# First attention in residue-class order with four key blocks a head, first scores among the transposes, and two more buffers for the late modulation units

## The chip, the cores and the metric

The kernel runs on one core of a Trainium2 chip. The metric is the device time of one execution in microseconds (us), the median of several runs.

## What is computed

One launch computes a whole layer of 256 tokens by 1024 channels, and then a second layer (a mixer, a memory cross-attention and a mixture of experts). The change touches only the middle of the first layer. What matters of its reference:

```python
DIL_GROUPS = ((128, 1), (512, 4), (2048, 16))      # (window, dilation); 4 heads of 64 channels in each group
...
def dilated_window_attention(q, k, v, window, dilation):
    """Each query i attends to keys i + dilation*m, |m| <= window/(2*dilation)."""
...
    mod = jax.nn.silu(c) @ w_ada + b_ada            # six rows of 1024, used to shift, scale and gate
    h = rms_norm(x, norm1_g) * (1 + sc1) + sh1
    proj = h @ w_in
    qa, ka, va, qb, kb, vb, gl = jnp.split(proj, IN_SPLITS, axis=-1)
    ...
    for gi, (win, dil) in enumerate(DIL_GROUPS):    # first attention: 12 heads
        o, l = dilated_window_attention(qa[:, :, sl], ka[:, :, sl], va[:, :, sl], win, dil)
    ...
    oa = softmax over the three groups' lse, times their outputs, summed
    branch_a = oa.reshape(b, s, DIL_OUT) @ w_proj_a
    ob = differential_attention(q1, q2, k1, k2, vb, lam)   # second attention: 8 heads
```

With 256 tokens, the group of dilation 4 reaches every key of the query's class modulo 4, and the group of dilation 16 every key of its class modulo 16. Only the group of dilation 1 has a band (64 tokens to either side). The three groups' softmax and the mixing by their denominators come to one softmax over the concatenated scores of one head of each group.

## The kernel before, in words

Weights come as units of 128 x 2048 numbers (1 MB) from one stream in memory. SP issues the loads. For a weight in TensorE's split precision, ACT makes a rounded copy (`hi`, L721), DVE the rest (`lo`, L1278), and TensorE (PE) multiplies three times (`mm3`, L2389 to L2391). Every engine runs an order that is written out by hand, with semaphores between them.

The stage around the change is this. The projection ends with unit U_PA - 1. Then PE transposes the queries and keys of both attentions (L2580), four blocks of 128 x 128 to a PSUM bank, 14 groups `g`; ACT copies the even groups to `qkT` (L871), DVE the odd ones (L1586). The last wait before the first scores is for all 14 copies.

The first attention has 8 steps `i` (4 slots, 2 halves of 128 queries; one step takes one head of each of the three groups). Of a step:
- `a_scores(i)` (PE, L2598): three products of 128 queries by 256 keys, 768 score columns in two PSUM banks
- `a_mask(i)` (DVE, L1594, L1597, L1599): scale and add the mask, take the maximum, negate it
- `a_exp(i)` (ACT, L877): the exponential in place, with the sum
- `a_transposes(i)` (PE, L2609): six 128 x 128 transposes to banks 4 and 5, which are free only when the step before has been copied
- the copy of these (ACT, L885), 768 columns, `a_pT`
- `a_values(i)` (PE, L2619): six products with the values, accumulated in bank 6
- `a_inverse(i)` (L1607) and `a_rows(i)` (L1613) on DVE: one over the sum, and the output rows

PE's order in step `i` is transposes(i), scores(i + 2), values(i - 1), `ada_half(1, i + 1)`. DVE's is inverse(i), `ada_sum(8 + i)`, mask(i + 2), rows(i - 1). In the last two steps the second attention's scores (L2631) and maxima (L1619, L1623) stand in for scores and mask. Before step 0, PE does scores(0), scores(1) and `ada_half(1, 0)`.

`ada_half` (L2496) and `ada_sum` (L1358, and L1360 for the first of eight) work off the late modulation units: 16 units `k` = 0 to 15 of the matrix `w_ada`, one in each step of the first attention and one in each of the 8 heads of the second (`ada_half(2, h)`, `ada_sum(16 + h)`). PE takes some columns of a unit, DVE the rest. These units lie in the two buffers `raw[:, 0 or 1, :]`; SP issues the load of unit `k` (L571) when both engines are done with `k - 2`. Behind unit 15 come U_PA and U_PB, the weights of the next products, into `spare` (L574), and further units into `raw` (L580). U_PA needs `hi`, `lo`, and then the transposed first attention (`T_OA`: ACT L768, DVE L1295) before PE goes on.

The second attention's heads begin on DVE with `b_weights` (L1647 to L1653). Its PE work is scores (L2631), transposes (L2662), values (L2674) and `ada_half`.

The masks are built by DVE between the projection's `lo` operations (L1446 to L1455). POOL only issues a few DMAs here. `H` (128 x 2 x 1024) is free from the first transposes of the projection until `b_rows` of the second attention writes it.

## Time and profile before

| | |
|---|---|
| median of 3 runs | 1825.12 us (1824.62 to 1835.89) |
| the profiled execution | 1830.13 us, of which the span is 1828.3 us |
| PE, DVE, ACT, POOL busy | 98%, 74%, 52%, 11% of the span |
| mean granted TensorE clock | 0.996 of full speed |
| PE transposes of queries and keys begin | 199.0 us after the span's start |
| step 0 of the first attention begins on PE | 211.0 us |
| the second attention's `b_weights(0)` begins on DVE | 249.8 us |
| PE's first product with U_PA | 289.2 us |

Times in the text are us from the start of the span. Busy shares are averages over the whole program; the rows further down are of the 90 us that the change touches.

### The profile page before, as it was taken

To read this page: it belongs to the slowest core of one execution; us is meant where nothing else is said; L and a number is where in the kernel's file an instruction comes from. 1 tells how busy PE (TensorE), PEld (TensorE's weight loads), DVE (VectorE), ACT (ScalarE), POOL (GpSimd) and SP (SyncE) were. 2 spreads that over 40 slices of the span, in tenths; PEclk is the share of its full clock that TensorE was granted. 3 is DMA by queue.
4 is the path that set the end of the run, shared out by engine and by line. 5 is a ranking of instruction groups with operands and counts; after the bars stand their busy time and mean duration, and the time that the engine had idled before them with its cause. 6 is when DMAs were issued, how large, how long until landed. Compare 5 with 4: busy or idle time off the path is not lost.

```text
span 1828.3 us, 25528 instructions
## 1 busy us (share of the span) xinstructions
PE 1791.1 (98%) x10036; PEld 1530.1 (84%) x10036; DVE 1355.7 (74%) x1887; ACT 952.2 (52%) x1035; POOL 197.5 (11%) x165
## 2 busy tenths in 40 slices
PE   8999999999999999999999999999999999999998
PEld 3788766899999988888888888898979888888886
DVE  5679687679589966666666666667874788888897
ACT  2543564454444444444444444456644567667665
POOL 0000000187700014441000000000000000000000
PEclk9999999999999999999999999999999999999999
DMA  8655365564445468886555555555343688898894
GB/s 316 253 184 185 132 224 188 199 234 174 185 157 205 188 235 276 289 293 225 185 195 193 184 186 195 193 189 182 134 151 145 237 329 344 332 353 330 324 354 171
DMA packets 65296, 413.55 MB, mean 226 GB/s; under 512 B 8641, under 2 KB 8929, under 8 KB 18865
## 3 DMA queue, kind: packets, MB, share of 16 engines
q1 hardware_dynamic: 51904, 371.22, 55.0%
q0 software_dynamic: 7248, 25.01, 4.0%
q10 hardware_dynamic: 6050, 16.02, 2.2%
q8 instruction: 64, 1.05, 0.2%
q14 instruction: 30, 0.25, 0.0%
HBM read 395.45 MB, written 16.78 MB: 225 GB/s over the span
## 4 chain that ended last, share of the span: by engine, by line
PE 88%; DVE 6%; DMA 3%; ACT 2%; issue 1%; SPq 0%; DVEq 0%; ACTq 0%
PE ps L2389 23%; PE ps L2391 22%; PE ps L2390 22%; PE ps L2766 6%; PE ps L2795 3%; PE ps L2768 3%; DVE wlo L1278 2%; DMA BIG<-in_stream_dram 1%; ACT whi L721 1%; PE ps L2978 1%; DMA raw<-in_stream_dram 1%; PE ps L2496 1%; PE ps L2619 1%; PE ps L2598 1%; PE ps L2856 1%
## 5 line engine op out<-in xcount | busy, mean ns | idle before, releaser
L1278 DVE TENSOR_TENSOR wlo<-raw,whi 128x2048 fp32r<-128x2048 f32 x181 | 414.7, 2291 | 208.4 <-ACT whi L721 208.2
L721 ACT ACTIVATE whi<-raw 128x2048 fp32r<-128x2048 f32 x181 | 346.8, 1916 | 368.3 <-PE ps L2391 241.7
L2389 PE MATMUL ps<-whi,phi 128*128 128x512 f32 x608 | 238.1, 392 | 2.3 <-DVE plo L1874 2.3
L2391 PE MATMUL ps<-whi,plo 128*128 128x512 f32 x608 | 237.2, 390 | 0.0
L2390 PE MATMUL ps<-wlo,phi 128*128 128x512 f32 x608 | 237.1, 390 | 0.0
L2389 PE MATMUL ps<-whi,tboth 128*128 128x512 f32 (+1 forms) x576 | 227.3, 395 | 6.9 <-DVE wlo L1278 4.0
L2389 PE MATMUL ps<-tboth,whi 128*128 128x256 f32 x768 | 221.6, 289 | 2.9 <-DVE tboth L1295 2.8
L2391 PE MATMUL ps<-whi,tboth 128*128 128x512 f32 (+1 forms) x576 | 223.9, 389 | 0.0
L2390 PE MATMUL ps<-wlo,tboth 128*128 128x512 f32 (+1 forms) x576 | 223.6, 388 | 0.0
L2391 PE MATMUL ps<-tboth,wlo 128*128 128x256 f32 x768 | 217.7, 283 | 0.0
L2390 PE MATMUL ps<-tboth,whi 128*128 128x256 f32 x768 | 217.7, 283 | 0.0
L2766 PE MATMUL ps<-tboth,whi 128*128 128x512 f32 x480 | 169.4, 398 | 0.0
L2389 PEld LDWEIGHTS ps<-tboth,whi 128*128 128x128 f32 x768 | 147.4, 192 | 4.2 <-issue 4.2
L2390 PEld LDWEIGHTS ps<-tboth,whi 128*128 128x128 f32 x768 | 147.5, 192 | 0.0
L2391 PEld LDWEIGHTS ps<-tboth,wlo 128*128 128x128 f32 x768 | 147.3, 192 | 0.0
L2389 PEld LDWEIGHTS ps<-whi,tboth 128*128 128x128 f32 x576 | 108.7, 189 | 32.8 <-DVE wlo L1278 5.2
L2389 PEld LDWEIGHTS ps<-whi,phi 128*128 128x128 f32 x608 | 114.2, 188 | 26.0 <-issue 3.7
L2391 PEld LDWEIGHTS ps<-whi,plo 128*128 128x128 f32 x608 | 114.2, 188 | 24.0
L2390 PEld LDWEIGHTS ps<-wlo,phi 128*128 128x128 f32 x608 | 114.3, 188 | 23.8
L2391 PEld LDWEIGHTS ps<-whi,tboth 128*128 128x128 f32 x576 | 108.6, 188 | 22.3
L2390 PEld LDWEIGHTS ps<-wlo,tboth 128*128 128x128 f32 x576 | 108.8, 189 | 21.6 <-issue 0.5
L2768 PE MATMUL ps<-tboth,wlo 128*128 128x256 f32 x420 | 118.1, 281 | 0.0
(435 smaller groups left out, 3313.3 us busy)
## 6 DMA issues: line engine op xcount, KB each, us to landing
raw<-in_stream_dram SPq DMA_DIRECT2D x249, 1024.0 KB, 4.8
BIG<-in_stream_dram SPq DMA_DIRECT2D x90, 1024.0 KB, 6.5
BIG<-g_spill POOLq DMA_DIRECT2D x64, 128.0 KB, 4.6
s_spill<-MOD ACTq DMA_DIRECT2D x28, 256.0 KB, 2.1
H<-in_stream_dram SPq DMA_DIRECT2D x6, 1024.0 KB, 4.9
BIG<-in_stream_dram SPq DMA_DIRECT2D x2, 2048.0 KB, 16.5
g_spill<-H ACTq DMA_DIRECT2D x4, 1024.0 KB, 5.4
g_spill<-MOD ACTq DMA_DIRECT2D x4, 1024.0 KB, 5.3
```

The source lines that it names most:

```text
L721: nc.scalar.activation(hi_of(u), raw_of(u), ACT.Copy).then_inc(unit_hi, 1)
L1278: nc.vector.tensor_tensor(wlo[:, u % 2, :], raw_of(u), whi[:, u % 2, :].bitcast(f32), ALU.subtract).then_inc(unit_split, 1)
L2389: nc.tensor.matmul(out, ahi, bhi, start=start, stop=False)
L2390: nc.tensor.matmul(out, ahi, blo, start=False, stop=False)
L2391: return nc.tensor.matmul(out, alo, bhi, start=False, stop=stop)
L2496: last = nc.tensor.matmul(ps[:, (7, 6)[g - 1] + m, :], silu_wide[:, c, :], raw[:, at % 2, m * 512:(m + 1) * 512], start=c == 0, stop=c == ...
L2598: last = nc.tensor.matmul(sc[:, k * S:(k + 1) * S], qkT[part, hd // 2, t * P:(t + 1) * P], qkT[part, 6 + hd // 2, :], start=True, stop=True)
L2619: last = nc.tensor.matmul(ps[:, 6, 0:HD], a_pT[b][:, k * P:(k + 1) * P], proj[:, k % 2, V0 + hd * HD:V0 + (hd + 1) * HD], start=k == 0, st ...
L2766: last = nc.tensor.matmul(out, whi[:, s, cols], both, start=c == 0, stop=c == DC - 1)
L2768: nc.tensor.matmul(out[:, 0:S], wlo[:, s, cols], thi[:, c, :], start=False, stop=False)
L2795: last = nc.tensor.matmul(out[:, q * N_KEYS:(q + 1) * N_KEYS], one_a[k][:, q, :], one_b[k][:, q, :], start=True, stop=True)
L2856: last = nc.tensor.matmul(ps[:, 4 + 2 * (l % 2) + t, h * P:(h + 1) * P], ks[:, h, kt * P:(kt + 1) * P], qs[:, h, qt * P:(qt + 1) * P], sta ...
```

## The change: what it does

1. **Class order.** Tokens are reordered by residue modulo 4, as the columns of `qkT` of the first attention: position (r, a) holds token 4a + r. The 128 queries of half `t` are then the classes 2t and 2t + 1. The groups of dilation 4 and 16 need only the 128 keys of the same half; the band group still takes all 256. A step has 512 score columns in one PSUM bank instead of 768 in two, four transposes instead of six, four products with the values instead of six. The transposes alternate between banks 4 and 5.
2. **Reordering costs.** The copies of the first six groups (blocks of the first attention's queries and keys) and the two operations of `T_OA` are strided (every fourth element). The values are moved into the new row order by eight DMAs on POOL, each 32 partitions by 768 numbers, from `proj` to `H`; they wait for the projection's block 12, and PE's first `a_values` waits for them (`v_moved`). The masks are built in the new order, with two small operations more and four operations of half the width.
3. **The sign.** The scores are negated with the masks, so that DVE's reduction is a minimum and is the bias itself; the operation on L1599 falls away, and `a_exp` has scale -1.
4. **The order before step 0.** After 8 of the 14 transpose groups PE waits for the copies of the first six and does scores(0) and scores(1); then the other six groups. DVE does mask(0) ahead of its copies 9, 11, 13; ACT does exp(0) behind its copy 8, ahead of copies 10 and 12.
5. **Buffers.** The late units 2, 3, 6, 7, 10 and 11 go to `late_units`, which lies over `whi` (free between the last unit of the projection and U_PA). Units 2 and 3 are issued when the projection's last units are used; units 4 to 13 when unit `k - 4` is used; units 14 and 15 when `k - 2` is used, as before.
6. **Semaphores.** `b_gate` and the late part of `b_ada` share one; DVE's block 7 waits for both.

The diff, cut to its core:

```diff
+CLASSES = A_DIL[1]
+QKT_FIRST, QKT_ALL = 8, QK_W // P // 4 * TT
...
+        with nc.sbuf_tensor("late_units", [P, 2, UW], f32) as late_tensor:
+            late_units = late_tensor
         whi = sb("whi", [P, 2, UW], f32r)
...
+        v_class = H[:, :, 0:A_W]
...
+        def by_class(cols):
+            return cols.rearrange("p c (a r) -> p c r a", r=CLASSES)
+        def qkT_rows(b4, t):
+            out, got = qkT[:, 4 * b4:4 * b4 + 4, :], ps[:, 4 + (TT * b4 + t) % 4, :].rearrange("p (b t) -> p b t", b=4)
+            if 4 * b4 >= 2 * A_W // P:
+                return out[:, :, t * P:(t + 1) * P], got
+            n = P // CLASSES
+            return out.rearrange("p b (r a) -> p b r a", r=CLASSES)[:, :, :, t * n:(t + 1) * n], by_class(got)
...
+        def late_of(at):
+            k = at - (U_PA - ADA_LATE)
+            return (late_units[:, at % 2, :] if k % 4 >= 2 and k < ADA_LATE - 2 else raw[:, at % 2, :])
...
             for u in range(late + 1, U_PA):
-                sp.wait_ge(unit_split, u - 1 - SPLIT_0)
-                if u - 2 >= late:
-                    sp.wait_ge(ada_used, u - 1 - late)
-                sp.dma_start(raw[:, u % 2, :], stream[u, :, :]).then_inc(raw_loaded[u % 2], 16)
+                k = u - late
+                if k >= 2:
+                    sp.wait_ge(raw_loaded[u % 2], landed(u - 2))
+                if k in (2, 3):
+                    sp.wait_ge(unit_used, U_PA - 4 + k - SPLIT_U + 1)
+                else:
+                    freed = u - 2 if k < 2 or k >= ADA_LATE - 2 else u - 4
+                    sp.wait_ge(unit_split, freed + 1 - SPLIT_0)
+                    if freed >= late:
+                        sp.wait_ge(ada_used, freed + 1 - late)
+                sp.dma_start(late_of(u), stream[u, :, :]).then_inc(raw_loaded[u % 2], 16)
...
+            pool.wait_ge(acc_free, 2 * ((V0 + A_W) // 512 + 1))
+            n = P // CLASSES
+            for r in range(CLASSES):
+                to, r2 = r // TT, r % TT * (P // 2)
+                for t in range(TT):
+                    pool.dma_start(v_class[r2 + t * n:r2 + (t + 1) * n, to, :], proj[r:P:CLASSES, t, V0:V0 + A_W]
+                                   ).then_inc(v_moved, 16)
...
+            for g in range(0, QKT_FIRST + 2, 2):
+                qkT_copy(g)
             a_exp(0)
+            for g in range(QKT_FIRST + 2, QKT_ALL, 2):
+                qkT_copy(g)
...
+                    if t == T_OA:
+                        nc.vector.tensor_tensor(by_class(tlo[:, chunks, tokens]), ps[:, tr_bank(t, k), :].rearrange(
+                            "p (c r a) -> p c r a", c=TT, r=CLASSES), by_class(thi[:, chunks, tokens].bitcast(f32)),
+                            ALU.subtract).then_inc(tr_lo, 1)
...
-                mark(nc.vector.scalar_tensor_tensor(a_s[b], sc, HD ** -0.5, masks[:, t * S:t * S + 768],
+                mark(nc.vector.scalar_tensor_tensor(a_s[b], ps[:, 2 * b, :], -(HD ** -0.5), masks[:, t * S:t * S + 512],
                                                     ALU.mult, ALU.add))
                 settle()
-                mark(nc.vector.tensor_reduce(a_max[:, b:b + 1], a_s[b], axis=AX.X, op=ALU.max))
-                settle()
-                nc.vector.tensor_scalar(a_nmax[:, b:b + 1], a_max[:, b:b + 1], -1.0, None,
-                                        ALU.mult).then_inc(a_masked, 1)
+                nc.vector.tensor_reduce(a_nmax[:, b:b + 1], a_s[b], axis=AX.X, op=ALU.min).then_inc(a_masked, 1)
...
+            for g in range(1, QKT_FIRST, 2):
+                qkT_copy(g)
             a_mask(0)
+            for g in range(QKT_FIRST + 1, QKT_ALL, 2):
+                qkT_copy(g)
             a_mask(1)
...
+                for g in a_groups(t):
+                    keys = rows if g else slice(0, S)
+                    n = keys.stop - keys.start
+                    last = nc.tensor.matmul(ps[:, 2 * b, at:at + n], qkT[part, hd // 2, rows],
+                                            qkT[part, 6 + hd // 2, keys], start=True, stop=True)
...
-                if i:
-                    pe.wait_ge(a_trT, i)
-                for k in range(6):
+                if i >= 2:
+                    pe.wait_ge(a_trT, i - 1)
+                for k in range(4):
...
+                else:
+                    pe.wait_ge(v_moved, 16 * CLASSES * TT)
                 pe.wait_ge(a_trT, i + 1)
...
+            for g in range(QKT_FIRST):
+                qkT_transposes(g)
+            pe.wait_ge(qkT_even, 2 * A_W // P // 4)
+            pe.wait_ge(qkT_odd, 2 * A_W // P // 4)
             a_scores(0)
             a_scores(1)
+            for g in range(QKT_FIRST, QKT_ALL):
+                qkT_transposes(g)
+            pe.wait_ge(qkT_even, QKT_ALL // 2)
+            pe.wait_ge(qkT_odd, QKT_ALL // 2)
             pe.wait_ge(silu_spread, 1)
             ada_half(1, 0)
```

## Rows read from the trace of the kernel before

**Rows 1.** Chain that ended last, from 199 us: start, duration, what, instructions.

```profile
199.15 6.13 PE ps L2580 x56
...
222.19 0.66 PE ps L2609 x6
222.85 1.49 PE ps L2598 x6
224.34 1.48 PE ps L2619 x12
225.82 0.91 PE ps L2496 x2
...
264.28 0.89 PE ps L2674 x8
...
271.23 4.85 DMA raw<-in_stream_dram
276.10 8.19 DMA spare<-in_stream_dram
...
288.55 0.61 DVE tboth L1295
```

**Rows 2.** Timeline of DVE in the first attention: start, duration, instruction, idle before.

```profile
222.88 0.16 DVE L1607 RECIPROCAL SM<-SM 128x1 f32<-128x1 f32 x1 [0.24 <-PE ps L2609]
222.97 1.95 DVE L1358 SCALAR_TENSOR_TENSOR BIG<-raw,SM,BIG 128x1024 f32<-128x1024 f32 x2
224.83 0.95 DVE L1594 SCALAR_TENSOR_TENSOR BIG<-ps,MOD 128x768 f32<-128x768 f32 x1
...
226.80 0.15 DVE L1599 TENSOR_SCALAR SM<-SM 128x1 f32<-128x1 f32 x1
226.88 0.28 DVE L1613 TENSOR_SCALAR BIG<-ps,SM 128x64 f32<-128x64 f32 x1
...
241.04 0.16 DVE L1607 RECIPROCAL SM<-SM 128x1 f32<-128x1 f32 x1 [0.26 <-PE ps L2609]
...
245.16 0.16 DVE L1607 RECIPROCAL SM<-SM 128x1 f32<-128x1 f32 x1
...
249.84 0.17 DVE L1647 RECIPROCAL SM<-SM 128x4 f32<-128x4 f32 x1
```

**Rows 3.** Timeline between the transposes and step 0, DVE, ACT and PE.

```profile
201.81 0.69 DVE L1586 COPY MID<-ps 128x512 f32<-128x512 f32 x1 [0.18 <-PE ps L2580]
...
205.48 1.28 ACT L877 ACT_TABLE_LOAD   x1
...
206.14 2.07 PE L2598 MATMUL ps<-MID 64*128 64x256 f32 x12 [0.88 <-DVE MID L1586]
...
210.96 1.29 PE L2609 MATMUL ps<-ident,BIG 128*128 128x128 f32 x6 [1.69 <-ACT BIG L877]
```

**Rows 4.** Busy time by window: PE, PEld, DVE, ACT, POOL; granted clock, DMA share, GB/s.

```profile
212.00:213.00 1.00, 1.00 (x4) 0.73 (x3) 0.71 (x2) 1.00 (x3) 0.00 (x0) 0.50 0.00 0
```

**Rows 5.** Groups by line and form, whole span: busy, mean ns, idle before.

```profile
L1619 DVE TENSOR_REDUCE SM<-ps 128x4 f32<-128x1024 f32 x8 | 9.8, 1223 | 1.8 <-PE ps L2631 1.8
...
L1716 DVE TENSOR_REDUCE MID<-MID 128x128 f32<-128x1024 f32 x1 | 2.0, 1986 | 0.0
```

**Rows 6.** Timeline of ACT: the evacuation of block 12, and the table load before L863.

```profile
184.44 1.06 ACT L729 ACTIVATE BIG<-ps 128x512 f32<-128x512 f32 x2
...
194.54 1.28 ACT L863 ACT_TABLE_LOAD   x1
195.84 3.71 ACT L863 ACTIVATE BIG<-BIG 128x2048 f32<-128x2048 f32 x2
```

**Rows 7.** Timeline of POOL at 677 us: two DMA issues of 128 KB.

```profile
677.38 1.77 POOL L677 DMA_DIRECT2D BIG<-g_spill  x2 [4.64 <-DVE MID L1867]
```

**Rows 8.** DMA issues: count, KB each, median us from issue to landing.

```profile
BIG<-g_spill POOLq DMA_DIRECT2D x64, 128.0 KB, 4.6
...
MOD<-in_b_ada_dram POOLq DMA_DIRECT2D x1, 2048.0 KB, 10.4
```

More of the change, by code:

```diff
@@ L767, in tr_high @@
                     act.wait_ge(tr_done, g + 1)
+                    if t == T_OA:
+                        nc.scalar.activation(by_class(thi[:, chunks, tokens]), ps[:, tr_bank(t, k), :].rearrange(
+                            "p (c r a) -> p c r a", c=TT, r=CLASSES), ACT.Copy).then_inc(tr_hi, 1)
+                        continue
                     nc.scalar.activation(thi[:, chunks, tokens], ps[:, tr_bank(t, k), :].rearrange(
@@ L884, in _ @@
                 act.wait_ge(a_tr, i + 1)
-                nc.scalar.activation(a_pT[i % 2], ps[:, 4:6, :].rearrange("p a n -> p (a n)")[:, 0:768], ACT.Copy
-                                     ).then_inc(a_trT, 1)
+                nc.scalar.activation(a_pT[i % 2], ps[:, 4 + i % 2, :], ACT.Copy).then_inc(a_trT, 1)
             def b_copy(h):
@@ L2574, in _, with qkT_transposes @@
             pe.wait_ge(acc_free, 2 * -(-(QK_W + GL_W) // 512))
-            for g in range(NQK // 4 * TT):
+            def qkT_transposes(g):
                 t, b4 = g % TT, g // TT
@@ L2593, in a_scores @@
                     pe.wait_ge(a_masked, i - 1)
[L2594 to L2595 removed]
+                rows, at = slice(t * P, (t + 1) * P), 0
+                for g in a_groups(t):
                     hd = g * A_SLOTS + h
                     part = slice(HD * (hd % 2), HD * (hd % 2) + HD)
[L2598 to L2599 removed]
+                    keys = rows if g else slice(0, S)
+                    n = keys.stop - keys.start
+                    last = nc.tensor.matmul(ps[:, 2 * b, at:at + n], qkT[part, hd // 2, rows],
+                                            qkT[part, 6 + hd // 2, keys], start=True, stop=True)
+                    at += n
                 last.then_inc(a_scored, 1)
@@ L2615, in a_values @@
                     pe.wait_ge(a_out, i)
+                else:
+                    pe.wait_ge(v_moved, 16 * CLASSES * TT)
                 pe.wait_ge(a_trT, i + 1)
-                for k in range(6):
-                    hd = a_groups(t)[k // 2] * A_SLOTS + h
+                for k, (g, keys) in enumerate((g, keys) for g in a_groups(t) for keys in ((t,) if g else range(TT))):
+                    hd = g * A_SLOTS + h
                     last = nc.tensor.matmul(ps[:, 6, 0:HD], a_pT[b][:, k * P:(k + 1) * P],
-                                            proj[:, k % 2, V0 + hd * HD:V0 + (hd + 1) * HD], start=k == 0, stop=k == 5)
+                                            v_class[:, keys, hd * HD:(hd + 1) * HD], start=k == 0, stop=k == 3)
                 last.then_inc(a_pv, 1)
```

76 lines of the change are left out of this document (38 added, 38 removed).

## The prediction

> **What bounds the kernel now.** I read the chain of work that ended last first. PE holds 88% of it over the whole program, so a change counts only where it shortens PE's own order or a wait of PE. Then I cut the chain to the 90 us of the change, and beside it the timelines of DVE, ACT, POOL and PE.
>
> In the first attention the chain is PE alone: transposes 0.66, scores 1.49, values 1.48, `ada_half` 0.91, which makes 4.54 us a step [rows 1]. DVE is nearly as long. It starts a step with the inverse at 222.88 and has its rows done at 226.88 + 0.28 = 227.16, so 4.28 of 4.54 us; the rest is a wait for PE of 0.24 [rows 2]. So PE can win only 0.3 us a step before DVE binds, unless DVE shrinks too.
>
> Ahead of step 0 PE is bare twice: 0.88 us for the last copy before the scores, and 1.69 us for exp(0) [rows 3]. Behind that PE runs at half clock: 0.50 at 212 us, which is 1.2 of 2.4 GHz [rows 4]. The six transposes at 210.96 took 1.29 where a later step shows 0.66 [rows 1, 3].
>
> At the stage's end the chain is two transfers, unit 15 at 271.23 and then into `spare` at 276.10 (4.85 and 8.19 us) [rows 1]. This is 13 us in which PE's speed counts for nothing. But unit 14 starts when unit 12 is used, unit 15 when unit 13 is used, and U_PA when 14 has landed, before and after the change. So that tail hangs on the second attention's fifth and sixth head and moves with them.
>
> **Steady steps.** PE after: four transposes of six, 0.66 x 4/6 = 0.44. Scores are one product of 256 columns and two of 128. A 256-column one is 1.49/3 = 0.50; a 128-column one is 0.89/4 = 0.22, from the second attention's values (eight instructions are four products) [rows 1]. That makes 0.94. Values 1.48 x 4/6 = 0.99, `ada_half` 0.91 unchanged. Sum 3.28, 1.26 less.
>
> DVE after: inverse to `ada_sum` 0.09; `ada_sum` to mask 1.86; the two passes over 768 columns now take 226.80 - 224.83 = 1.97 [rows 2]. A pass over 512 is 0.69, against 0.95 [rows 2, 3], so 1.97 - 0.52 = 1.45. The negation on L1599 goes, which is 0.08 up to the next start. Rows 0.28. Sum 3.68, less some 0.1 of overlap at the end: 3.6 us. **DVE becomes the bound of the step**, and I count 4.54 - 3.6 = 0.94 and not 1.26. ACT's step (768-column exponential and copy) only gets shorter and lies beside.
>
> From the inverse of step 2 (222.88) to `b_weights(0)` (249.84) is 26.96 us [rows 2]. Steps 2 to 5: 4 x 3.6 = 14.4. Step 6 was 245.16 - 241.04 = 4.12; after, DVE has 0.09 + 1.95 + 0.2 + 1.22 (the maxima, rows 5) + 0.15, so 3.6. Step 7 was 4.68; DVE's 3.6 and then rows(7) 0.25 make 3.85. Sum 21.85, **gain 5.1 us**.
>
> **The start.** Transposes take 6.13/14 = 0.44 us a group from 199.0 [rows 1]. Copy 5 starts at 201.81 and ends at 202.50 [rows 3]; PE is through group 7 at 202.5, so scores(0) starts at 202.65 without a stop. It takes 0.94. Scores(1) adds 0.4, as the twelve instructions took about 2.0 and not 3.0 [rows 3]. Groups 8 to 13 then need 6 x 0.44, to 206.7. DVE: mask(0) 203.7 to 205.1, copies 9, 11, 13 to 207.5, mask(1) to 208.9. ACT: copy 8 to 205.2, then **the table load of 1.28 us**, which in the kernel before lay in ACT's idle time behind the last copy [rows 3] and now holds up copies 10 and 12: 206.5, exp(0) to 207.3, copies to 208.45. PE waits for copy 12 from 206.7 to 208.5, then `ada_half(1, 0)` 0.91, and step 0 starts at 209.5 instead of 210.96. So scores-first by itself brings 1.5 us only: the wait for exp(0) turns into one for ACT's copies.
>
> The rest of the start follows by the same durations. DVE inverse(0) 210.0, `ada_sum(8)` 1.13, mask(2) to 212.65, inverse(1), `ada_sum(9)` to 214.6, mask(3) and rows(0) to 216.4. So the inverse of step 2 comes at 216.45 instead of 222.88, **gain 6.4 us**, of which about 3 are the half clock that the kernel before paid on 210.96 to 217 (1.29 for 0.66, and likewise scores and `ada_half`).
>
> The Trainium skill, ScalarE: Activation LUTs, "What ACT_TABLE_LOAD costs", says that a switch of tables costs a drain of about 1.38 us beside the 1.28. By that rule ACT's copies would be at 209.8, and the gain 1.4 us smaller. Here the load before L863 begins at 194.54 and its operation at 195.84 [rows 6], so behind the load nothing but its 1.28 shows, and I leave the drain out.
>
> **Strided operations.** No row shows a stride of four elements. Bounds: nothing, or the factor of the one slow strided reduction, 1986 against 1223 ns for 1024 elements [rows 5], on a 0.69 copy +0.4. It bears on copies 1, 3, 5 of DVE (the scores then start at most 0.8 later) and on `T_OA`'s 0.61 at 288.55, which PE waits for [rows 1]; ACT's are covered. I take 0.4 + 0.2 = **0.6 us**, nearer the low end, since that row strides 128 elements; the range keeps 0 and 1.2.
>
> The Trainium skill, SBUF, "Door 1: The DMA port swizzle", says that SBUF is read in lines of 16 bytes and a stride of four floats is still free. By it the cost would be 0; no row here shows this.
>
> **Moved values.** They wait for block 12, evacuated at 184.44 + 1.06 = 185.5 [rows 6]. POOL issues two DMAs of 128 KB in 1.77 us [rows 7], so eight in 7.1, and such a one lands after 4.6 [rows 8]: 197.2. PE asks for them in values(0) at about 213.7. They cost nothing while that 16 us cover holds. Behind PE's wait lie `ada_half(1, 2)` and all later steps. Beside them in the DMA engines are only units 0 to 3, which have until 209.
>
> **Buffers.** Each unit now has two steps more, 7.2 us, to land; 4.85 is needed [rows 1]. With two buffers and steps of 3.6 it would have been near. Cost 0, gain 0 on today's path: the chain has no transfer within the first attention. **Masks** (two small operations more, 0.15 each; four of half width, less 0.13 each) and the shared semaphore (2 MB landed 10.4 us after its issue at 49 us [rows 8], asked for after 110): 0, between operations of DVE that wait for ACT there. The second attention is untouched, with its values where they were.
>
> **Sum.** 5.1 + 6.4 - 0.6 = 10.9 us on the profiled execution, 1830.1 to 1819.2. That execution is 5.0 us above the median; I carry the difference over: 1825.1 - 10.9 = **1814.2 us**.
>
> **Rivals.**
> - Half clock again (chance 0.25). After the change PE still stands 1.8 us for ACT's copies, in one piece, where before it stood 0.88 and 1.69. If the clock falls again, `ada_half`, transposes and scores of steps 0 and 1 take twice their time, some 3 us: 1817.2. The same holds if the kernel before does not fall in its unprofiled runs.
> - The gain is given back in a wait for data (0.08). If units land late at 3.6 us a step, or the transfers into `spare` set the end by themselves, only the start's gain stays, or less: 1825.1 - 3 = 1822. Against it: the chain shows issues that follow use.
> - DVE overlaps better than its starts show, PE binds (0.1): steps of 3.3 us, 2 more: 1812.
> - The class order doesn't relieve the step, because DVE's strided or PSUM-bound passes stay at 768's time (0.03): 1819 to 1820.
> - Slower (0.04). The eight value copies are one after another, not overlapped: their place is PE's wait in values(0), the decision falls at (213.7 - 185.5)/8 = 3.5 us each. At 10.4 us each, the slowest POOL landing [rows 8], they end at 268.7, 55 us late, net +44: 1869. At 4.6 each it is 222.3, 8.6 late, and 1823. Against it: POOL issued L677's pairs without waiting for a landing [rows 7].
>
> **How the numbers follow.** The forecast has 0.50. The range 1810 to 1821 takes in the clock rival, PE's bound, both ends of the strides and some 2 us of spread; out are the data wait and the slow side. Faster by over 1% would need 18.3 us, more than PE's 1.26 x 8 and all bare time of the start together: 0.05. Slower by over 1% only by the last rival: 0.03. About 1% is what a measurement of this kernel can tell from no change, so the likely outcome counts as the same, 0.92.
>
> **What would show it.** Steps of 3.6 us, with DVE's idle gone and PE idle 0.3 a step; ACT's table load between its copies 8 and 10, and step 0 at 209.5; clock 1.00 at 212; POOL's eight issues from 185.5; `b_weights(0)` near 238.9; the two transfers at the end 13 us long as before. The prediction is wrong if PE is idle more than 0.4 us a step for a semaphore of DVE, or if values(0) waits for `v_moved`.

## The result, and the profile after

The changed kernel took **1816.8 us** in the median of 7 runs (1815.79 to 1817.76). The kernel before took 1826.71 beside it (7 runs, 1824.62 to 1835.89). The ratio is 0.9934, with a 95% interval of [0.9916, 0.9951]. The ratio makes about 12 us, the medians make 9.9, against 10.9 predicted. It is under 1%, so by the prediction's own line the two count as the same. The time lies 2.6 us above the forecast of 1814.2 and inside its range. The profiled execution took 1816.28 us, its span 1814.2, at a mean granted clock of 0.999; in the kernel before it was 1830.13, 1828.3 and 0.996.

The 14.1 us between the two spans, by marks that both traces have:

| stretch | before | after | less |
|---|---|---|---|
| start to the transposes of queries and keys | 198.99 | 198.71 | 0.28 |
| to the inverse of step 2 | 23.89 | 17.49 | 6.40 |
| to `b_weights(0)` | 26.96 | 21.83 | 5.13 |
| to PE's first product with U_PA | 39.36 | 39.23 | 0.13 |
| to the end of the span | 1539.10 | 1536.94 | 2.16 |

The 0.13 us are the sum of two things: the two transfers at the end of the stage took 0.51 us less than before, and `T_OA` on DVE took 0.38 us more (both below).

**The start.** The timeline of PE, ACT and DVE in the changed kernel, from ACT's copy 8 to step 0 (start, duration, instruction, idle before it and what ended that):

```profile
204.64 0.60 ACT L912 ACTIVATE MID<-ps 128x512 f32<-128x512 f32 x1 [2.08 <-PE ps L2633]
...
205.25 1.28 ACT L916 ACT_TABLE_LOAD   x1
...
206.55 0.72 ACT L916 ACTIVATE BIG<-BIG,SM 128x512 f32<-128x512 f32 x1
...
207.27 1.06 ACT L912 ACTIVATE MID<-ps 128x512 f32<-128x512 f32 x2
...
208.38 1.13 PE L2549 MATMUL ps<-raw,MOD 128*128 128x512 f32 x2 [1.60 <-ACT MID L912]
...
209.35 0.60 PE L2661 MATMUL ps<-ident,BIG 128*128 128x128 f32 x4
```

The table load stands between copy 8 (204.64) and exp(0), and copies 10 and 12 (207.27) stand behind both. PE's last wait before step 0, 1.60 us, ends with them. Step 0 begins at 209.35 instead of 210.96 [rows 3], and the clock stays up. Busy time by window, in the columns of [rows 4], at 212 and 290 us:

```profile
212.00:213.00 1.00, 1.00 (x8) 0.77 (x7) 0.97 (x3) 0.45 (x1) 0.00 (x0) 1.00 0.92 131
290.00:291.00 1.00, 1.00 (x6) 0.84 (x5) 1.00 (x2) 0.00 (x0) 0.00 (x0) 1.00 0.00 0
```

The kernel before had 0.50 at 212, and a second such stretch, from about 290 to 293, that my prediction had not looked for:

```profile
290.00:293.00 3.00, 3.00 (x8) 2.33 (x8) 2.97 (x5) 1.34 (x1) 0.00 (x0) 0.50 0.31 131
```

What this second stretch cost can be read from the first copy of `tboth` on ACT behind PE's product with U_PA, in the chains of three kernels: the kernel before, the changed kernel, and e3 (below), which is the kernel before with another order ahead of step 0 and has no low clock here:

```profile
298.77 0.70 ACT tboth L768
```

```profile
285.27 0.70 ACT tboth L809
```

```profile
292.28 0.70 ACT tboth L768
```

Counted from the product (289.20, 277.26 and 284.30) it comes after 9.57, 8.01 and 7.98 us. So the second stretch at half clock cost 1.6 us in that execution, and most of the 2.16 in the last row of the table is this.

**A step.** The timeline of DVE in steps 2 and 3 of the changed kernel:

```profile
216.20 0.16 DVE L1656 RECIPROCAL SM<-SM 128x1 f32<-128x1 f32 x1
216.30 1.95 DVE L1405 SCALAR_TENSOR_TENSOR BIG<-late_units,SM,BIG 128x1024 f32<-128x1024 f32 x2
218.16 0.68 DVE L1646 SCALAR_TENSOR_TENSOR BIG<-ps,MOD 128x512 f32<-128x512 f32 x1
218.88 0.69 DVE L1649 TENSOR_REDUCE SM<-BIG 128x1 f32<-128x512 f32 x1
219.48 0.28 DVE L1662 TENSOR_SCALAR BIG<-ps,SM 128x64 f32<-128x64 f32 x1
219.86 0.16 DVE L1656 RECIPROCAL SM<-SM 128x1 f32<-128x1 f32 x1
...
238.03 0.17 DVE L1700 RECIPROCAL SM<-SM 128x4 f32<-128x4 f32 x1
```

No operation of a step has an idle time behind it in brackets: from 216.20 to 219.86 DVE works without a stop, 3.66 us. In the kernel before, the chain of this stretch was PE from end to end [rows 1]; now it is DVE.

**The end of the stage**, in the same chain: unit 15, then the transfer into `spare`, then `hi`, `lo`, `T_OA` and PE.

```profile
259.42 4.81 DMA raw<-in_stream_dram
...
264.24 7.72 DMA spare<-in_stream_dram
...
276.22 0.99 DVE tboth L1333
...
277.26 0.50 PE ps L2442
```

The two transfers last 12.5 us, 13.0 before [rows 1], and begin 11.8 us earlier. The 0.5 us are no effect of the change that any run shows: in e1, which has the same transfers, they last 11.5. DVE's part of `T_OA` takes 0.99 here instead of 0.61.

### The profile page after: what moved, and what is told of

It is laid out like the page before. It is cut to its first block, busy times and chain, and to the rows that moved or that the text cites. A ratio compares the mean times of both kernels' runs of the same rounds, so it can differ in the third digit from the quotient of the medians.

```text
span 1814.2 us, 25435 instructions
## 1 busy us (share of the span) xinstructions
PE 1778.0 (98%) x9988; PEld 1519.4 (84%) x9988; DVE 1349.9 (74%) x1881; ACT 949.5 (52%) x1035; POOL 201.8 (11%) x173
## 3 DMA queue, kind: packets, MB, share of 16 engines
q8 instruction: 64, 1.05, 0.2%
## 4 chain that ended last, share of the span: by engine, by line
PE 86%; DVE 7%; DMA 3%; ACT 2%; issue 1%; SPq 0%; DVEq 0%; ACTq 0%
PE ps L2442 23%; PE ps L2444 22%; PE ps L2443 22%; PE ps L2828 6%; PE ps L2857 3%; PE ps L2830 3%; DVE wlo L1320 2%; DMA BIG<-in_stream_dram 1%; ACT whi L758 1%; PE ps L3040 1%; DMA raw<-in_stream_dram 1%; DVE BIG L1405 1%; PE ps L2918 1%; DVE H L1359 1%; PE ps L2549 0%
## 5 line engine op out<-in xcount | busy, mean ns | idle before, releaser
L758 ACT ACTIVATE whi<-raw 128x2048 fp32r<-128x2048 f32 x181 | 346.8, 1916 | 367.7 <-PE ps L2444 241.9
```

Source lines behind the costliest of these rows:

```text
L758: nc.scalar.activation(hi_of(u), raw_of(u), ACT.Copy).then_inc(unit_hi, 1)
```

## The experiments

All times of marks are relative to the first transpose of queries and keys in the same trace, so that what happens earlier in a run drops out. "Product" is PE's first product with U_PA. Each kernel has one profiled execution, whose span stands in the table. The kernel before that ran beside the experiments had medians of 1827.25 to 1829.37. A "fall" is a stretch at half clock, 0.50 in the windows.

| kernel | inverse 0 | inverse 2 | `b_weights(0)` | product | span | median (runs) | ratio to before, 95% |
|---|---|---|---|---|---|---|---|
| before | 13.30 | 23.89 | 50.85 | 90.21 | 1828.3 | 1826.71 (7) | |
| after | 11.27 | 17.49 | 39.32 | 78.55 | 1814.2 | 1816.8 (7) | 0.9934 [0.9916, 0.9951] |
| e1, order undone | 11.30 | 17.52 | 39.37 | 77.56 | 1814.1 | 1816.62 (6) | 0.9944 [0.9931, 0.9956] |
| e2, before with PE busy | 12.87 | 21.04 | 48.20 | 87.46 | 1826.4 | 1826.41 (11) | 0.9992 [0.9984, 1.0001] |
| e3, before with order only | 12.13 | 20.03 | 46.92 | 85.66 | 1823.3 | 1824.53 (11) | 0.9984 [0.9974, 0.9993] |
| e4, table early | 10.48 | 16.70 | 38.54 | 77.19 | 1813.9 | 1816.07 (5) | 0.9938 [0.9925, 0.9952] |
| e5, two buffers | 11.28 | 18.97 | 46.67 | 85.77 | 1822.2 | 1825.65 (12) | 0.9998 [0.9986, 1.001] |
| e6, less DVE | 11.29 | 17.30 | 38.42 | 77.29 | 1815.8 | 1817.98 (6) | 0.9946 [0.9933, 0.9959] |
| e7, less PE | 11.28 | 17.35 | 42.13 | 80.89 | 1818.8 | 1817.58 (6) | 0.9943 [0.9931, 0.9955] |
| e8, values in place | 11.28 | 17.50 | 39.34 | 78.32 | 1817.2 | 1818.4 (6) | 0.9945 [0.9931, 0.9959] |
| e9, `T_OA` in order | 11.28 | 17.50 | 39.34 | 78.53 | 1814.9 | 1816.74 (6) | 0.9936 [0.9921, 0.9951] |
| e10, four to the end | 11.28 | 17.50 | 39.35 | 77.61 | 1813.5 | 1815.62 (6) | 0.9932 [0.9917, 0.9946] |
| e11, three together | 10.48 | 16.70 | 38.78 | 76.05 | 1813.6 | 1815.95 (6) | 0.993 [0.9914, 0.9945] |
| e12, before with four buffers | 12.88 | 20.78 | 47.57 | 85.37 | 1822.6 | 1826.01 (12) | 0.9994 [0.9983, 1.0006] |

**The kernel before by clock.** Each timed run has its own mean granted clock. Over the four groups of runs that the experiments brought, the kernel before has 67 (a 68th, of 6318 us, is left out):

| clock | 0.995 | 0.996 | 0.997 | 0.998 | 0.999 |
|---|---|---|---|---|---|
| runs of before | 10 | 9 | 15 | 15 | 16 |
| their median, us | 1831.5 | 1830.0 | 1828.6 | 1826.8 | 1825.4 |

The two that the table leaves out are slower still (1835.9 at 0.993, 1834.7 at 0.994). So a thousandth of mean clock goes with about 1.5 us. The profiled execution of before had 0.996, and its 1830.13 is the time that belongs to that clock. The changed kernel's 7 runs lie at 0.997 to 0.999. Its three at 0.999 have the median 1816.1, so 9.3 us less than before's at the same clock.

**e1, order undone.** The changed kernel, with all 14 groups and copies before the first scores, as in the kernel before:

```diff
-            for g in range(QKT_FIRST):
+            for g in range(QKT_ALL):
                 qkT_transposes(g)
-            pe.wait_ge(qkT_even, 2 * A_W // P // 4)
-            pe.wait_ge(qkT_odd, 2 * A_W // P // 4)
+            pe.wait_ge(qkT_even, QKT_ALL // 2)
+            pe.wait_ge(qkT_odd, QKT_ALL // 2)
             a_scores(0)
             a_scores(1)
-            for g in range(QKT_FIRST, QKT_ALL):
-                qkT_transposes(g)
...
-            for g in range(0, QKT_FIRST + 2, 2):
+            for g in range(0, QKT_ALL, 2):
                 qkT_copy(g)
             a_exp(0)
```

> The changed kernel with part 4 undone: all 14 transpose groups and copies, then scores(0) and scores(1). Theory A (scores-first moved PE's wait from exp(0) to ACT's copies behind the table load, and brought next to nothing by itself): scores start 0.3 us earlier than the kernel before had them, 205.9; mask(0) 206.9 to 208.3, exp(0) to 209.2, step 0 at 209.3 to 209.6, against 209.35 with scores-first; total within 1 us of the changed kernel's 1816.8 where the clock stays up. Rival B (scores-first is what brought the start forward): step 0 at 210.9 or later and the total 1.5 to 3 us longer. Where the granted clock falls behind the two bare stretches, some 3 us come on top in that run.

Measured: inverse 0 at 11.30 instead of 11.27, and every later mark the same within 0.05 us until `b_weights(0)`. ACT's and PE's timeline:

```profile
205.73 1.28 ACT L916 ACT_TABLE_LOAD   x1
...
208.99 0.72 ACT L916 ACTIVATE BIG<-BIG,SM 128x512 f32<-128x512 f32 x1 [1.97 <-DVE SM L1647]
...
209.85 0.66 PE L2657 MATMUL ps<-ident,BIG 128*128 128x128 f32 x4 [0.76 <-ACT BIG L916]
```

With all copies first, the table load is hidden (it ends at 207.01, and exp(0) comes at 208.99), and masks and exponentials of 512 columns instead of 768 bring step 0 nearly as early, with its inverse at the same time. What scores-first gains on PE, ACT's queue of load, exp(0) and two copies takes back.

e1 shows one thing more. Its product comes 0.99 us earlier than the changed kernel's (77.56 against 78.55), although nothing behind `b_weights(0)` was edited: the chain has 4.71 and 6.77 us for the two transfers, and 4.81 and 7.72 in the changed kernel. So differences of up to 1 us in the column "product" can be the transfers alone.

**e2, before with PE busy.** The kernel before, with four short products on idle operands after `ada_half(1, 0)`, to keep PE from standing:

```diff
             ada_half(1, 0)
+            run_on(6, 4)
             for i in range(n_a):
                 a_transposes(i)
```

> The kernel before with four idle products of 128 x 256 on PE between ada_half(1, 0) and step 0, some 1.9 us, where PE stood for exp(0). They are extra work whose result is not used. Theory A (about 3 us of the gain at the start were the half clock behind that stretch): granted clock 1.00 at 212, step 2's inverse some 3 us earlier than 222.9 although step 0 may begin 0.2 us later, and a median 2 to 4 us below the kernel before. Rival B (the half clock was hidden behind DVE, or doesn't happen in unprofiled runs): no difference in the median, or slightly slower.

Measured: no fall at 212, and inverse 2 comes 2.85 us earlier. From there on the chain has a new piece:

```profile
213.14 5.07 DMA raw<-in_stream_dram
...
218.25 1.12 PE ps L2496 x2
```

With the start at full clock, unit 2 is late: it is asked for at 213.12, when DVE is done with unit 0, and lands at 218.21. PE stands only 0.22 us for it. So in the kernel before the slow clock hid a short wait for two buffers. At clock 0.999 its six runs have the median 1825.5, the kernel before's 1825.4. What e2 takes away is therefore only what an execution with the fall pays, and by the overall ratio that is 1 to 2 us on average (0.9992; its interval reaches from 3 us to nothing), less than the 2 to 4 of theory A.

**e3, before with order only.** The kernel before with part 4 of the change alone: eight groups, their copies, scores(0) and scores(1), then the other six; ACT's exp(0) behind copy 8, DVE's mask(0) behind copy 7.

```diff
+            for g in range(8):
+                qkT_transposes(g)
+            pe.wait_ge(qkT_even, 3)
+            pe.wait_ge(qkT_odd, 3)
             a_scores(0)
             a_scores(1)
+            for g in range(8, NQK // 4 * TT):
+                qkT_transposes(g)
```

> The kernel before with part 4 alone: its 768-column scores after 8 of the 14 transpose groups, masks and exp(0) among the copies. Theory A (ACT's table load and copies are the end of the start): mask(0) 204.2 to 206.1, exp(0) 206.8 to 207.9, copies 10 and 12 to 209.1, step 0 at 210.1, 0.9 us earlier than 210.96; 1 us by itself, 3 more if the clock stays up. Rival B (the order brings the whole overlap of transposes and scores): step 0 near 208.5, 2.5 us without the clock.

Measured: inverse 0 is 1.17 us earlier and the clock does not fall in the stage; inverse 2 is 3.86 earlier. Not all of the 1.17 is the order: without the fall the kernel before has its inverse 0 at 12.87 (e2) or 12.88 (e12) instead of 13.30, because the first six transposes are then not at half clock. That leaves 0.75 us for the order. None of its 11 runs has a clock under 0.998, where 36 of before's 67 have one. At 0.999 its median is 1824.5, 0.9 under before's. So in the kernel with long masks the new order is worth 0.8 to 0.9 us by itself, and with it the low clocks did not come; why they did not is open.

**e4, table early.** The changed kernel, with one exponential of 128 numbers between ACT's copies 6 and 8, so that the table is loaded while ACT waits for PE:

```diff
-            for g in range(0, QKT_FIRST + 2, 2):
+            for g in range(0, QKT_FIRST, 2):
                 qkT_copy(g)
+            nc.scalar.activation(warm, pidx, ACT.Exp, scale=-1.0)
+            qkT_copy(QKT_FIRST)
             a_exp(0)
```

> The changed kernel with one small exponential on ACT between its copies 6 and 8, so that the table load of 1.28 us falls into ACT's idle 2.08 us. Theory A (the table load between the copies is what PE waits for ahead of step 0): exp(0) at 205.3, copies 10 and 12 done at 207.1, step 0 at 208.1 instead of 209.35, the total 1.2 us shorter: 1815.6 against 1816.8. Rival B (mask(1) and DVE's copies are next and as late): step 0 earlier but the inverse of step 2 within 0.4 us of 216.2, total unchanged.

Measured, from the timeline of ACT and PE:

```profile
202.71 1.28 ACT L921 ACT_TABLE_LOAD   x1
...
204.77 0.60 ACT L912 ACTIVATE MID<-ps 128x512 f32<-128x512 f32 x1 [0.56 <-PE ps L2635]
205.26 0.71 ACT L916 ACTIVATE BIG<-BIG,SM 128x512 f32<-128x512 f32 x1
...
207.75 1.10 PE L2551 MATMUL ps<-raw,MOD 128*128 128x512 f32 x2 [0.83 <-ACT MID L912]
```

Exp(0) starts 1.42 us earlier, counted from the first transpose, yet PE's wait only halves, from 1.60 to 0.83: ACT now has to wait for PE's groups (0.56). The 0.79 us gained at inverse 0 arrives at `b_weights(0)` (38.54 against 39.32). The table load was half of the remaining wait, not all: theory A's 1.2 us did not come. The product comes 1.36 us earlier (77.19 against 78.55); the rest of that is the transfers again, which last 11.95 us here.

**e5, two buffers.** The changed kernel without part 5: all late units in `raw`, each issued when `k - 2` is used.

```diff
-            return (late_units[:, at % 2, :] if k % 4 >= 2 and k < ADA_LATE - 2 else raw[:, at % 2, :])
+            return raw[:, at % 2, :]
```

> The changed kernel with part 5 undone: all late units in raw, issued when k - 2 is used. Theory A (the shorter step needs the two buffers more): a load is issued at the end of ada_sum, lands 4.85 us later, then ada_half 0.91, transposes 0.44, and ada_sum 2.0 of the next but one step: 8.3 us for two steps, 4.15 a step instead of 3.66, some 3 us over steps 1 to 7; total 1819 to 1821. Rival B (my sum's value of nothing for the buffers, since two steps of 3.6 are more than 4.85): steps stay at 3.66 and the total at 1816.8.

Measured: `b_weights(0)` comes 7.35 us later than in the changed kernel, and the median is 1825.65. **Without the buffers nothing of the change is left** that the timed runs can show. It is 4.7 us above the upper end of theory A's 1819 to 1821. The chain shows one round of two steps after the other:

```profile
211.87 4.77 DMA raw<-in_stream_dram
...
216.69 1.12 PE ps L2545 x2
217.81 0.45 PE ps L2657 x4
...
218.37 1.96 DVE BIG L1401 x2
...
220.37 4.85 DMA raw<-in_stream_dram
...
225.27 2.08 PE ps L2545 x2
...
230.33 5.07 DMA raw<-in_stream_dram
```

The load starts when DVE has used the unit two before (211.87). PE stands until it has landed, does `ada_half` and the transposes of the next step; only then DVE may take its inverse and its own part of the unit (218.37 + 1.96), which frees the next load (220.37). These are 8.50 us for two steps against 7.32. In each of the rounds PE stands 1.46 or 1.47 us for the transfer. Behind the first of these waits the clock stays up, behind the second and third it falls (0.50 at 226 and 236 by the windows), `ada_half` takes 2.08 instead of 1.12, and the round takes 9.96. I had put 4.15 us on a step; it was 4.25 at full clock and 4.98 with the fall. None of its 12 runs has a clock above 0.996, where 46 of before's 67 do. Yet its seven at 0.996 have the median 1824.4 and before's nine 1830.0. So the shorter steps do save time at an equal mean clock, and low clocks in every run take it back; that PE's waits bring them is the likely reading, not a shown one.

**e6, less DVE** (leaves out DVE's smaller part of each late unit in the first attention) and **e7, less PE** (in six of the steps' units, PE multiplies 128 of the 512 columns).

```diff
+                if g == 1 and c:
+                    parts = tuple(parts)[:1]
                 for total, part in parts:
```

```diff
+                    n = 128 if g == 1 and 0 < c < DC - 1 else 512
-                    last = nc.tensor.matmul(ps[:, (7, 6)[g - 1] + m, :], silu_wide[:, c, :],
-                                            late_of(at)[:, m * 512:(m + 1) * 512], start=c == 0, stop=c == DC - 1)
+                    last = nc.tensor.matmul(ps[:, (7, 6)[g - 1] + m, 0:n], silu_wide[:, c, :],
+                                            late_of(at)[:, m * 512:m * 512 + n], start=c == 0, stop=c == DC - 1)
```

> The changed kernel with part of the computation left out: DVE's second operation of ada_sum in the first attention (512 columns of the modulation rows' sum), 0.61 us a step. Theory A (DVE bounds the step at 3.66 us, PE has 3.46): steps of 3.46, seven times 0.2 = 1.4 us shorter. Rival B (PE bounds): no change.

> The changed kernel with part of the computation left out: ada_half of the first attention takes 128 of its 512 columns in its middle six steps, 0.7 us of PE a step. Theory A (DVE bounds the step): steps stay at 3.66, total within 0.5 us. Rival B (PE bounds): steps 0.2 to 0.7 us shorter.

Measured in e6, DVE in the same two steps:

```profile
216.33 0.16 DVE L1658 RECIPROCAL SM<-SM 128x1 f32<-128x1 f32 x1 [0.57 <-PE ps L2663]
...
219.79 0.16 DVE L1658 RECIPROCAL SM<-SM 128x1 f32<-128x1 f32 x1 [0.57 <-PE ps L2663]
```

Now DVE idles 0.57 for PE, and the step takes 3.46: PE's side of it. In e7 the first steps stay at 3.66 (inverses at 216.39, 220.05 and 223.72). So DVE sets the step, by 0.2 us only. In e6 `b_weights(0)` comes 0.90 us earlier (1.4 predicted), but neither kernel's median fell. e7 even lost 2.8 us to `b_weights(0)`: PE, with less to do in a step and a wait of up to 0.78 us for DVE in it, was at half clock from 221.1 to 234.7, and the chain there is PE's, with the four transposes at 0.85 and not 0.60:

```profile
221.41 0.85 PE ps L2662 x4
...
226.69 0.85 PE ps L2662 x4
```

That is 5.28 us for a step, and the next took as long. So in the profiled execution an engine with less work became the slower one. That the missing work brought the long fall is not shown: of the six timed runs (median 1817.58) the profiled one has 0.994, two have 0.998 and three 0.999.

**e8, values in place.** No moves by POOL; `a_values` reads `proj` as it lies, so the first attention's values stand in the wrong rows.

```diff
-                    pool.dma_start(v_class[r2 + t * n:r2 + (t + 1) * n, to, :], proj[r:P:CLASSES, t, V0:V0 + A_W]
-                                   ).then_inc(v_moved, 16)
...
-                    v_class[:, keys, hd * HD:(hd + 1) * HD]
+                    proj[:, keys, V0 + hd * HD:V0 + (hd + 1) * HD]
```

> The changed kernel with part of the computation changed: the values are read from where the projection left them, in token order, and the eight DMAs and the wait for them are gone. Theory A (the moved values cost nothing, they land some 16 us ahead of their use and disturb no load): total within 0.5 us, step times equal. Rival B (their traffic delays the units or PE's operands): 1 us or more shorter.

Measured: all marks within 0.02 us of the changed kernel's until `b_weights(0)`. Its span is 3.0 us longer, and 2.89 of that lies ahead of the stage: a load landed at 62.85 instead of 60.89, and a fall followed at 67.9 to 71.3. Both come long before the moves. Its two runs at 0.999 have 1815.9. The moves cost nothing.

**e9, `T_OA` in order.** The two operations of `T_OA` read PSUM with the stride and write in order, in place of the other way round:

```diff
-                        nc.scalar.activation(by_class(thi[:, chunks, tokens]), ps[:, tr_bank(t, k), :].rearrange(
-                            "p (c r a) -> p c r a", c=TT, r=CLASSES), ACT.Copy).then_inc(tr_hi, 1)
+                        nc.scalar.activation(thi[:, chunks, tokens].rearrange("p c (a r) -> p c a r", r=CLASSES),
+                            ps[:, tr_bank(t, k), :].rearrange("p (c r a) -> p c a r", c=TT, r=CLASSES),
+                            ACT.Copy).then_inc(tr_hi, 1)
...
```

> The changed kernel with the two T_OA operations walking the other way: written to SBUF in order, read from PSUM with a stride of 64. Theory A (the stride of four on the SBUF side is what made them 1.13 and 1.05 us instead of 0.61 and 0.68; PSUM can be read at a stride for nothing, as in the copies): ACT's back to 0.6, DVE's to 0.69, the first product with U_PA 0.4 us earlier after DVE's lo. Rival B (the four-dimensional pattern costs, whichever side has the stride): both stay near 1.1.

The two operations in the timeline, first in the changed kernel, then in e9:

```profile
274.99 1.13 ACT L806 ACTIVATE tboth<-ps 128x512 fp32r<-128x512 f32 x1
276.15 1.05 DVE L1333 TENSOR_TENSOR tboth<-ps,tboth 128x512 fp32r<-128x512 f32 x1
```

```profile
275.89 0.61 ACT L806 ACTIVATE tboth<-ps 128x512 fp32r<-128x512 f32 x1
277.04 0.68 DVE L1336 TENSOR_TENSOR tboth<-ps,tboth 128x512 fp32r<-128x512 f32 x1
```

The stride costs 0.37 to 0.52 us on the side of SBUF and nothing on the side of PSUM. The product does not move (78.53): `T_OA` gives 0.38 us and the transfers 0.2, but e9 had a fall at 238.6 to 242.0, behind which the second attention runs 0.56 us later. And 0.4 us is under what the timed runs can tell.

**e10, four to the end.** Units 14 and 15 in the third and fourth buffer as well, and U_PA's successors freed by units 12 and 13; the copies of `hi(U_PA)` and `hi(U_PB)` then wait until `late_units` is free.

```diff
-            return (late_units[:, at % 2, :] if k % 4 >= 2 and k < ADA_LATE - 2 else raw[:, at % 2, :])
+            return (late_units[:, at % 2, :] if k % 4 >= 2 else raw[:, at % 2, :])
...
-                    freed = u - 2 if k < 2 or k >= ADA_LATE - 2 else u - 4
+                    freed = u - 2 if k < 2 else u - 4
...
-            for u, freed in ((U_PA + 2, U_PA - 2), (U_PA + 3, U_PA - 1), (U_PA + 4, U_PA + 2)):
+            for u, freed in ((U_PA + 2, U_PA - 4), (U_PA + 3, U_PA - 3), (U_PA + 4, U_PA + 2)):
...
+            act.wait_ge(ada_used, ADA_LATE - 1)
+            act.wait_ge(unit_split, U_PA - 1 - SPLIT_0)
             hi(U_PA)
```

> The changed kernel with the late units 14 and 15 in late_units too, issued when units 10 and 11 are used, U_PA + 2 and U_PA + 3 issued when 12 and 13 are used, and ACT waiting for the use of 14 and 15 before it writes over them. Theory A (the 13 us of transfers at the stage's end are the issue rule, not the memory): U_PA is there before ACT asks, hi(U_PA) begins behind b_rows(6) 1.6 us earlier, and head 7 doesn't wait 0.5 for unit 15; total 1.6 to 2.2 us shorter. Rival B (ACT's and DVE's order around hi(U_PA) holds it as late anyway): 0.5 us or less.

Measured: the 12.5 us of transfers are gone from the chain, and in their place stands the second attention itself:

```profile
266.66 1.72 PE ps L2553 x4
...
271.07 1.81 ACT whi L758
272.90 2.29 DVE wlo L1324
275.20 0.99 DVE tboth L1337
...
276.23 0.50 PE ps L2446
```

The product comes 0.94 us earlier, in spite of a fall at 238.5 to 241.9, behind which the second attention runs 0.82 us later than in the changed kernel. Without the fall it would be some 1.8 us (an estimate, their sum), in theory A's 1.6 to 2.2. So the transfers had been hiding work that ends 1 to 2 us sooner, not 12.5. The product is no earlier than e1's, though, where two shorter transfers did as much by chance, and the median is 1.2 us lower.

**e11, three together** (e4, e9 and e10 in one kernel).

> The changed kernel with the early table load, T_OA written in order and the late units in four buffers to the end. If the three pieces are independent: 1.2 + 0.4 + 1.9 = 3.5 us below the changed kernel, 1813.3. If one hides behind another: less than 2.5.

The product comes 2.5 us earlier than in the changed kernel, in spite of a fall at 236.7 to 240.1, which puts the second attention 0.4 behind e4's. The pieces sum to nearly that: 0.79 (e4), 0.38 (e9) and about 1.8 (e10), less 0.4. So they are independent, but smaller than the 3.5 that I had added up. The median is 1815.95, 0.85 under the changed kernel's, and the ratios to before, 0.993 and 0.9934, overlap. By the mark "product" it is the fastest of all versions; by the timed runs it can't be told from the changed kernel.

**e12, before with four buffers.** The kernel before with part 5 of the change alone: `late_units`, `late_of` and SP's rule for the issues, as in the change's diff.

```diff
-                sp.dma_start(raw[:, u % 2, :], stream[u, :, :]).then_inc(raw_loaded[u % 2], 16)
+                sp.dma_start(late_of(u), stream[u, :, :]).then_inc(raw_loaded[u % 2], 16)
```

> The kernel before with the four buffers for the late units alone (their choice and the rule by which their loads are given out); the first attention's steps stay as they were. Theory A (the buffers serve only the shorter step: with steps of 4.54 us TensorE sets the rate, and a unit given out when one is used lands in time): steps stay at 4.54 us, from the inverse of step 2 to the attention's weights of step 0 26.9 to 27.0 us (26.96 in the kernel before), and the median within 1.5 us of the kernel before's. Rival B (the buffers alone bring a good part of the 9 us that their removal took from the changed kernel): that stretch is shorter by over 1 us, and the median 3 us or more under the kernel before's.

Measured: from inverse 2 to `b_weights(0)` 26.79 us against 26.96, and 4.54 between the inverses of steps 5 and 6:

```profile
233.83 0.16 DVE L1621 RECIPROCAL SM<-SM 128x1 f32<-128x1 f32 x1 [0.26 <-PE ps L2623]
238.37 0.16 DVE L1621 RECIPROCAL SM<-SM 128x1 f32<-128x1 f32 x1 [0.26 <-PE ps L2623]
```

From step 4 on PE sets the step as before. The stretch is 0.11 us shorter than theory A's 26.9 to 27.0, and far from the 1 us of rival B. The ratio is 0.9994 [0.9983, 1.0006]; the medians differ by 3.4 us (1826.01 and 1829.37), but the 12 and 17 runs lie at different clocks. The three at 0.999 have the median 1824.4, and before's sixteen 1825.4. So the buffers alone bring at most 1 us. The trace has 0.26 of it by inverse 2 (20.78 against e2's 21.04), which is the wait of 0.22 for unit 2 that e2 laid bare.

## Why the prediction was right, and where it was off

**The bound of the step, and the 5.1 us.** The mechanism was right. DVE's sum was 3.68, and the trace has 3.66: the 0.1 taken off for overlap was not there. e6 shows that DVE sets the step and that PE follows 0.2 behind (3.46; predicted 3.28), and e7's first steps agree. From the inverse of step 2 to `b_weights(0)` the forecast was 21.85 and the trace has 21.83. So near a hit is luck: steps 2 to 5 took 14.65 instead of 14.4, steps 6 and 7 took 3.48 and 3.70 instead of 3.6 and 3.85, and the errors cancel.

**The start, and the 6.4 us.** The marks were right: step 0 at 209.35 (predicted 209.5), inverse of step 2 at 216.20 (216.45), gain 6.40; the table load where it was expected. The attribution was wrong: "scores-first by itself brings 1.5 us only". By e1 it brings nothing in this kernel. Masks and exponentials of 512 columns put step 0 equally early with all copies first. The two parts are two ways to the same 1.6 us (inverse 0 at 11.3 against 12.88 without the fall); e3 shows that the order is worth 0.75 us where the masks are long. I had credited the order with a saving that the shorter masks bring as well, and since only their sum showed, the sum came out.

**The half clock.** "About 3 are the half clock" was right for the profiled execution: e2 has 2.85 less. The forecast that the clock stays up was right too. But not every run of before pays it (16 of 67 ran at 0.999).

**The step that failed: "I carry the difference over".** The 5.0 us between before's profiled execution and its median was no fixed offset. It goes with falls of the clock: 0.996 in that execution, and 1.5 us for each thousandth. In the changed kernel's profile the fall at 211 to 218 is gone, and the one at 290 to 293 did not come either, which is 1.6 of the 2.16 us that the last stretch lost. Whether the change removed the second can't be said: e3, with nothing edited near it, did not have it either. So the correct sum goes either from profile to profile, 1830.1 less 10.9 and 2.2, which is 1817.0 (measured 1816.28), or between runs at 0.999, 1825.4 less 10.9 plus 3, which is 1817.5 (measured 1816.1 at 0.999). I had subtracted the gain of 3 us from a median that holds it only in part. The rival "half clock again" gave 1817.2, the nearest number, partly for this reason: I had written under it that it also holds if before does not fall in its unprofiled runs. Beside that, the median of three runs, 1825.12, was low: 1.6 us under that of the seven, 2.1 to 4.2 under those beside the experiments. With 1826.71 the same sum gives 1815.8, so 1.6 of the 2.6 us by which the forecast was low are the sample. That only 1.0 is left for the wrong step is luck as well: gains that the prediction did not have (the second fall, 0.5 us of transfers, 0.2 of strides) went the other way.

**Buffers.** "Cost 0, gain 0 on today's path" was right for the kernel before (e12), and the sentence beside it, "with two buffers and steps of 3.6 it would have been near", was far too mild: e5 loses 7.35 us to `b_weights(0)` and all of the median. I compared 7.2 us for two steps with 4.85 for a load. The round holds more than the load. It is load 4.77, `ada_half` 1.12, transposes 0.45, and DVE's own use 1.96, with the starts between them 8.50. **Neither everything but the buffers (e5, 0.9998) nor the buffers alone (e12, 0.9994) nor the order before step 0 alone (e3, 0.9984) brings more than 3 us; the class order with the buffers (e1) brings 0.9944, all that the whole change brings within the measurement.** What each would be worth "by itself" was the wrong question for all three.

**Strides.** Predicted 0.6: nothing on the copies and on the scores' start (DVE's copies still 0.69), 0.38 in the chain for `T_OA`. The bound of +0.4 for one operation was the right size, and I had halved it. The Trainium skill, SBUF, "Door 1: The DMA port swizzle", gives 4 fp32 as a stride that is still free. That does not hold for these two operations, on ACT and on DVE, which took 1.13 and 1.05 us against 0.61 and 0.68 in order. The same passage says that an access that crosses to a new line pays a penalty, and with this the two times agree; the prediction had left that half out.

**Moved values.** Cost 0 as predicted (e8). They began at 185.5 as predicted, and POOL's eight issues took 4.19 us and not 7.1:

```profile
185.51 4.19 POOL L684 DMA_DIRECT2D H<-BIG  x8 [136.22 <-ACT BIG L766]
```

So the slow side (eight one after another) did not come. By the table of DMA issues one lands 5.9 us after its issue in the median (4.6 predicted), the last at about 195.6, 18 us before PE's first values (213.51; predicted 213.7).

**The tail.** Two transfers of 12.5 us, moved with the second attention, as predicted; e10 shows that they hid nearly as much other work. Their time is not fixed: in the chains of before, after, e1, e4, e6, e8 and e9 it lies between 11.5 and 13.0 us, a spread over twice the 0.6 us that I had set for strides.

**The ScalarE drain.** By the Trainium skill's 1.38 us drain beside the load, exp(0) would have begun at 207.9. It began at 206.55, 0.02 after the load's end (205.25 + 1.28), and the load itself began 0.01 after copy 8 ended. So the load's 1.28 us of the Trainium skill, ScalarE: Activation LUTs, "What ACT_TABLE_LOAD costs", shows in the trace and the drain does not; e4's load (202.71, next operation 204.00) says the same.

Open: why the clock falls in one execution and not in the next of the same kernel. The runs show how often and what it costs, not the cause. Falls stand at other places in other profiles too (at 1188 us in e3, at 68 in e8), so none of the single profiles can tell whether an edit brought or removed one; only the clocks of many timed runs can, as for e3 and e5. Nor was the sign (part 3) or the class order without part 4 and part 5 run by itself.

## What to carry to other kernels

When a step is shortened, follow the whole round that frees a buffer (load, first user, last user, next issue) and not only the load against the number of steps; a buffer that is worth nothing at the old rate can hold the whole gain at the new one, so test each part of a change within the finished kernel and not only by itself. And before subtracting a gain from a median, look up the granted clock of every timed run: part of what a profile shows as gain may be a fall of the clock that many runs never had.

## What the runs showed of the hardware that I had not expected

- TensorE's mean granted clock differs from run to run of one kernel (0.993 to 0.999 over 67 runs of before), and a thousandth of it goes with 1.5 us of 1827. In one profile with less work on PE (e7) it was at half clock from 221.1 to 234.7, where the kernel with more work had no fall; that the one brought the other is not shown.
- One stretch at half clock, 290 to 293 us, cost 1.6 us; PE was busy in it throughout.
- A stride of four numbers on the SBUF side took ACT 1.13 and DVE 1.05 us for 128x512, in order 0.61 and 0.68; on the PSUM side the same stride, and in e9 a longer one, cost nothing.
- The twelve instructions of scores(0) and scores(1), the first six on one half of the rows and the last six on the other, took 2.07 us together before [rows 3] and 1.65 after with a third of the columns gone; the six of a later step alone take 1.49 [rows 1]. So two steps' scores back to back overlap.
